# The head of a hybrid decoder kernel: x transposed before it is normalised, 1/rms applied from a row at eviction

## The chip, the cores and the metric

The kernel runs on one core of one Trainium2 chip. The metric is the device time of one execution in microseconds (us), lower is better. An execution that was taken with the hardware profiler gives the rows of this document.

## The reference, cut to what matters

The program is one layer of a hybrid decoder for 256 prompt tokens and 8 x 4 sample tokens, 288 columns in all, at a width of 2048. Everything starts with

```
h    = x * rsqrt(mean(x*x over the 2048) + 1e-6) * g_pre
proj = h @ w_in          # 2048 x (5*2048 + 16 + 5*2048)
```

The first columns of `proj` that the kernel makes are the 2048 of `vb`; then gates, an mLSTM branch and a gMLP branch, two further projections, an output projection and a last RMSNorm follow. All inputs and outputs are float32.

## The kernel before, in words

**Products.** The 104 weight pairs (256 columns each, `w_in`, `w_pb`, `w_pa`, `w_out`) are all done in one way. A pair comes in four chunks of 4 x 128 rows. SyncE loads a chunk into `raw`, ScalarE rounds it to `whi` (L800), VectorE makes the rest `wlo = raw - whi` (L1064), and TensorE does for each of the 4 x 128 rows k and each of the 2 x 128 columns three products over 288 tokens: `whi` by `xh`, `whi` by `xl`, `wlo` by `xh` (L440 to L442). `xh` and `xl` are the rounded upper and the lower part of the transposed, normalised x, 16 pieces (k = 0 to 15) of 128 x 288. They are made once, in the head, while the first pair runs, and used until the last branch.

**The head.** SyncE loads x in four pieces: prompt rows 0 to 127 (1 MB), the samples on 32 partitions, the two halves of prompt rows 128 to 255 (L359 to L362); then weights. TensorE runs idle matmuls (L456, `idle_run`) on the identity. Squares are summed by ScalarE (L817, L820) and VectorE (L1075, L1078); VectorE adds them (L1081, L1084), GpSimd takes the power -0.5 (L1655) into `rstd`. ScalarE (L825) and VectorE (L1093) then multiply x by `rstd`, in quarters of 512 columns, into `hb`; tokens are partitions there, so `rstd` is a scalar of each partition. TensorE transposes `hb` in 128 x 128 blocks, three a k (L474, L475), into PSUM. ScalarE evicts a k times `g_pre` into `xh` (L835); VectorE evicts the same bank once more and subtracts into `xl` (L1106). The first six k are transposed before the first product, the others one by one between the products of k = 1 to 10 (`x_piece`). VectorE's queue has the lower split of chunks 0 to 3 among these.

**Behind the first pair** come the gate sums (32 products, L483 and L484), the second pair with the transposes of `w_s` (L491) in it, and so on. The order of every engine is written out by hand; engines wait for each other by semaphores. GpSimd sets constants and masks at the start (memsets and selects, L1620 to L1651), issues the load of the gate weights `wg` (L1653), takes the power, issues four small loads, waits until all of x is transposed, makes further constants, and loads `wsn`, `bsb`, `lng`, `lnb`.

Of the kernel before, what the change touches and what calls it, by code (L numbers as in the profile page):

```python
# [26 lines left out]
F32 = mybir.dt.float32  # L27
# [5 lines left out]
P = 128  # L33
D = 2048
# [19 lines left out]
SQ = D // 4  # L54
LO = 32
# [43 lines left out]
def build(nc, x_prompt, x_sample, state_C, state_n, state_m, state_conv, g_pre, w_in, b_ig, b_fg,  # L99
# [35 lines left out]
    xpart = fixed("xpart", [P, 3])  # L135
# [14 lines left out]
    xt = a("xt", [P, 3, D])  # L150
    hb0 = a("hb0", [P, 3, D])
    prow = a("prow", [P, 2, P])
    a = Area(phase)
# [118 lines left out]
    def sem(name):  # L272
# [9 lines left out]
    x_norm_a, x_in_rest, x_sum = sem("x_norm_a"), sem("x_in_rest"), sem("x_sum")  # L282
# [4 lines left out]
    x_sq, x_var, x_rstd, x_norm, x_t, x_hi, x_lo = (sem(n) for n in (  # L287
        "x_sq", "x_var", "x_rstd", "x_norm", "x_t", "x_hi", "x_lo"))
# [60 lines left out]
    def x_bank(k):  # L349
        return 2 + k % 6  # L350
# [76 lines left out]
    def _(pe):  # L427
        def chunk(pair, c, slot, free, mh_, ml_, pieces=None):
# [25 lines left out]
        def idle_run(n):  # L454
            for _ in range(n):
                nc.tensor.matmul(ps[:, 7, 0:P], ident[:], ident[:], start=True, stop=True)  # L456

        pe.wait_ge(consts, 1)
        idle_run(28)
        pe.wait_ge(par_in, 64)  # L460
        pe.transpose(ps[:, 6, 0:P], prow[:, 0, :], ident[:])
        pe.transpose(ps[:, 6, P:P + 64], prow[0:64, 1, :], ident[0:64, 0:64]).then_inc(par_t, 1)
        def turn_x(k0, k1):

            for k in range(k0, k1):
# [1347 lines left out]
```

## Time and profile before

| what | us |
|---|---|
| median of 3 runs | 1482.71 |
| lowest and highest of them | 1482.71, 1483.03 |
| the profiled execution, its own time | 1483.09 |
| its span, first to last instruction | 1481.6 |
| TensorE busy | 1466.3 |
| VectorE busy | 880.8 |
| ScalarE busy | 620.1 |
| GpSimd busy | 190.6 |

Times within rows count from the start of the span. PE is TensorE, PEld its weight load, DVE VectorE, ACT ScalarE, POOL GpSimd, SP SyncE. A matmul's recorded duration overlaps that of the next; what one costs is read from start to start. An idle matmul on float32 has two records.

### The profile page before, as it was taken

The page shows a single profiled execution, that of the slowest core. Times are in us where ns is not written, and L with a number is a line of the kernel's source. Part 1 is how long each engine was busy: PE and PEld are TensorE (multiplying, and loading weights), DVE is VectorE, ACT ScalarE, POOL GpSimd, SP SyncE. Part 2 cuts the span into 40 slices and gives each one's busy share as a digit, 9 for nine tenths or more (in the row PEclk, how much of TensorE's full clock was granted, in tenths as well). Part 3 has the DMA queues.
Part 4 walks back from the last instruction along what each step waited for, and adds up shares of the span by engine and source line. Part 5 has one row for each costly group of instructions (what it writes and reads, how often), then busy time and mean ns, then how long its engine had stood idle before and what let it go on. Part 6 is the DMA issues. An engine that isn't in the chain of part 4 may idle for free. (4 is left out here: it accounts for less than half of the span.)

```text
span 1481.6 us, 31209 instructions
## 1 busy us (share of the span) xinstructions
PE 1466.3 (99%) x11131; PEld 1448.1 (98%) x11131; DVE 880.8 (59%) x1451; ACT 620.1 (42%) x869; POOL 190.6 (13%) x340
## 2 busy tenths in 40 slices
PE   9999999999999999999999999999999999999996
PEld 9999999999999999999999999999999999999996
DVE  7756565564434447676767677777767544545444
ACT  6433333333333334444544444544453343333442
POOL 4000000001000000304040404040412100000000
PEclk9999999999999999999999999999999999999998
DMA  7764655557555568696969696979796665655543
GB/s 230 222 160 134 181 154 169 167 145 244 185 171 179 176 188 213 160 297 162 300 167 292 166 296 171 288 184 281 185 277 166 210 184 169 183 174 187 173 157 138
DMA packets 310678, 292.14 MB, mean 197 GB/s; under 512 B 82880, under 2 KB 297608, under 8 KB 309840
## 3 DMA queue, kind: packets, MB, share of 16 engines
q1 hardware_dynamic: 291424, 243.05, 59.1%
q0 software_dynamic: 18960, 48.48, 9.7%
q8 instruction: 24, 0.39, 0.1%
q10 hardware_dynamic: 256, 0.10, 0.0%
q14 instruction: 14, 0.11, 0.0%
HBM read 266.11 MB, written 25.44 MB: 197 GB/s over the span
## 5 line engine op out<-in xcount | busy, mean ns | idle before, releaser
L1064 DVE TENSOR_TENSOR wlo<-raw,whi 128x1024 fp32r<-128x1024 f32 x416 | 507.7, 1223 | 534.2 <-ACT whi L800 529.1
L440 PE MATMUL ps<-xh,whi 128*128 128x288 f32 x2560 | 762.3, 298 | 0.0
L442 PE MATMUL ps<-xh,wlo 128*128 128x288 f32 x2560 | 755.5, 295 | 0.0
L441 PE MATMUL ps<-xl,whi 128*128 128x288 f32 x2560 | 754.5, 295 | 0.0
L800 ACT ACTIVATE whi<-raw 128x1024 fp32r<-128x1024 f32 x416 | 440.4, 1059 | 748.8 <-PE ps L442 718.7
L440 PEld LDWEIGHTS ps<-xh,whi 128*128 128x128 f32 x2560 | 481.4, 188 | 6.9 <-issue 6.2
L442 PEld LDWEIGHTS ps<-xh,wlo 128*128 128x128 f32 x2560 | 480.6, 188 | 0.0
L441 PEld LDWEIGHTS ps<-xl,whi 128*128 128x128 f32 x2560 | 480.3, 188 | 0.2
L441 PE MATMUL ps<-yl,whi 128*128 128x288 f32 x512 | 151.5, 296 | 0.0
L440 PE MATMUL ps<-yh,whi 128*128 128x288 f32 x512 | 150.8, 294 | 0.0
L442 PE MATMUL ps<-yh,wlo 128*128 128x288 f32 x512 | 150.6, 294 | 0.0
L442 PEld LDWEIGHTS ps<-yh,wlo 128*128 128x128 f32 x512 | 96.2, 188 | 0.0
L440 PEld LDWEIGHTS ps<-yh,whi 128*128 128x128 f32 x512 | 96.2, 188 | 0.0
L441 PEld LDWEIGHTS ps<-yl,whi 128*128 128x128 f32 x512 | 96.1, 188 | 0.0
L440 PE MATMUL ps<-mh,whi 128*128 128x288 f32 x248 | 73.5, 296 | 0.0
L441 PE MATMUL ps<-ml,whi 128*128 128x288 f32 x248 | 73.4, 296 | 0.0
L442 PE MATMUL ps<-mh,wlo 128*128 128x288 f32 x248 | 73.1, 295 | 0.0
L1736 POOL DMA_DIRECT2D out_dram<-cst x64 | 36.1, 564 | 219.0 <-DVE cst L1431 214.2
L1361 DVE SCALAR_TENSOR_TENSOR Cin<-Cin,dec_bc,ps 128x512 f32<-128x512 f32 x64 | 46.3, 744 | 0.6
L440 PEld LDWEIGHTS ps<-mh,whi 128*128 128x128 f32 x248 | 46.6, 188 | 0.0
L441 PEld LDWEIGHTS ps<-ml,whi 128*128 128x128 f32 x248 | 46.6, 188 | 0.0
L442 PEld LDWEIGHTS ps<-mh,wlo 128*128 128x128 f32 x248 | 46.6, 188 | 0.0
(341 smaller groups left out, 1073.8 us busy)
## 6 DMA issues: line engine op xcount, KB each, us to landing
raw<-in_w_in_dram SPq DMA_DIRECT2D x320, 512.0 KB, 4.0
raw<-in_w_pb_dram SPq DMA_DIRECT2D x32, 512.0 KB, 3.5
Cin<-in_state_mlstm_C_dram POOLq DMA_DIRECT2D x16, 1024.0 KB, 8.7
Xb<-in_state_mlstm_C_dram SPq DMA_DIRECT2D x256, 64.0 KB, 3.8
out_dram<-Cin POOLq DMA_DIRECT2D x16, 1024.0 KB, 6.0
raw<-in_w_pa_dram SPq DMA_DIRECT2D x32, 512.0 KB, 3.5
raw<-in_w_out_dram SPq DMA_DIRECT2D x32, 512.0 KB, 3.5
bcs<-rows_d POOLq DMA_DIRECT2D x8, 304.0 KB, 3.9
```

The costliest lines, as they stand in the source:

```text
L440: nc.tensor.matmul(out, whi[:, c, kk, cols], mh_[:, k, :], start=(k == 0), stop=False)
L441: nc.tensor.matmul(out, whi[:, c, kk, cols], ml_[:, k, :], start=False, stop=False)
L442: last = nc.tensor.matmul(out, wlo[:, c, kk, cols], mh_[:, k, :], start=False, stop=(k == KT - 1))
L800: nc.scalar.activation(whi[:, c], raw[:, c], ACT.Copy).then_inc(hi_ready, 1)
L1064: nc.vector.tensor_tensor(wlo[:, c], raw[:, c], whi[:, c].bitcast(F32), ALU.subtract).then_inc(lo_ready, 1)
L1361: nc.vector.scalar_tensor_tensor(Cin[:, b], Cin[:, b], dec_bc[:, ds(8 * h + b, 1)], ps[:, NEW_BANK[b % 3], :].rearrange("p (v k) -> p v k" ...
L1736: pool.dma_start(blocks_of(conv_p_v, h, s, g), cst[g:g + 3, 2 * s:2 * s + 2, :]).then_inc(cst_out, 16)
```

## The change

x is transposed as it lands, before anything is known of its mean square. `hb` is gone.

- SyncE loads the first half of prompt rows 128 to 255 ahead of the samples, and the samples in four quarters of 512 columns onto the four groups of 32 partitions (`xs`).
- TensorE: 21 idle matmuls, transposes of k = 0 to 7 of the first 128 rows, 5 idle matmuls, the two transposes of parameters, those of k = 0 to 7 of the second 128 rows, 4 for all the samples, a matmul that adds the four partial sums of squares of a sample (`same_x`), 10 idle matmuls. The transposes of k = 8 to 15 are done in four calls of 4, ahead of the products of k = 2, 4, 6 and 8.
- `rstd` is brought to all partitions as a row of 288: VectorE multiplies the identity by it (`diag`), TensorE multiplies ones by that, ScalarE copies the result to `rbc`.
- VectorE makes `xn` (a ring of four pieces of 128 x 288 in SBUF) from PSUM times `g_pre` times `rbc`, in two instructions, 256 and 32 columns; ScalarE rounds it to `xh`; `xl = xn - xh` is made by VectorE for k = 0 and 1 and by GpSimd for k = 2 to 15.
- The products of a k in the first pair are in the order: four with `xh`, then two with `xl`; their waits are separate.
- VectorE does the memsets that GpSimd did; GpSimd does its later constants, the small loads and `wg` before the power, and `wsn` and `bsb` behind it, ahead of the subtractions; `lng` and `lnb` come behind them.

```
-        sp.dma_start(xt[0:S, 2, :], xs_v).then_inc(x_in[2], 16)
         sp.dma_start(xt[:, 1, HALVES[0]], xp_v[:, 1, HALVES[0]]).then_inc(x_in[1], 16)
+        for q in range(4):
+            sp.dma_start(xs[S * q:S * q + S, :], xs_v[:, SQ * q:SQ * q + SQ]).then_inc(x_in[2], 16)
...
         pe.wait_ge(consts, 1)
-        idle_run(28)
+        idle_run(21)
+        pe.wait_ge(x_in[0], 16)
+        for k in range(8):
+            turn_x(k, 0)
+        idle_run(5)
         pe.wait_ge(par_in, 64)
...
+        pe.wait_ge(x_in[1], 16)
+        for k in range(8):
+            turn_x(k, 1)
+        pe.wait_ge(x_in[2], 64)
+        for n in range(CK):
+            pe.transpose(ps[:, 7, P * n:P * n + P], xs[:, P * n:P * n + P], ident[:])
+        pe.wait_ge(xs_sq, 1)
+        pe.wait_ge(x_made, 3)
+        nc.tensor.matmul(ps[:, 6, 0:1], same_x[:], xpart[:, 3:4], start=True, stop=True).then_inc(xs_sum, 1)
+        idle_run(10)
+
+        def rstd_rows():
...
+            for t, n in enumerate((P, P, S)):
+                pe.wait_ge(x_made, t + 4)
+                last = nc.tensor.matmul(ps[:, 6, P * t:P * t + n], ones8[:], diag[:, P * t:P * t + n],
+                                        start=True, stop=True)
+            last.then_inc(rbc_mm, 1)
+
+        def turn_more(k):
+
+            pe.wait_ge(x_t, k - 6)
+            for kk in (k, k + 1):
+                for t in range(2):
+                    last = pe.transpose(x_prompt_t(kk)[:, P * t:P * t + P], xt[:, t, P * kk:P * kk + P], ident[:])
+            last.then_inc(x_more, 1)
+
+        def first_chunk(c):
+
+            pe.wait_ge(lo_ready, c + 1)
+            for kk in range(CK):
+                k = CK * c + kk
+                if k in (2, 4, 6, 8):
+                    turn_more(k + 6)
+                pe.wait_ge(x_hi, k + 1)
...
+                    nc.tensor.matmul(out, whi[:, c, kk, cols], xh[:, k, :], start=(k == 0), stop=False)
+                    nc.tensor.matmul(out, wlo[:, c, kk, cols], xh[:, k, :], start=False, stop=False)
+                if k < XL_DVE:
+                    pe.wait_ge(x_lo, k + 1)
+                else:
+                    pe.wait_ge(x_lo_p, k + 1 - XL_DVE)
+                for j in range(2):
+                    last = nc.tensor.matmul(ps[:, j, 0:T], whi[:, c, kk, P * j:P * j + P], xl[:, k, :],
+                                            start=False, stop=(k == KT - 1))
...
+        act.wait_ge(x_in[2], 64)
+        nc.scalar.activation(junk_s[:, 0:SQ], xs[:], ACT.Square, accum_out=xpart[:, 3:4]).then_inc(xs_sq, 1)
+        act.wait_ge(xs_sum, 1)
+        nc.scalar.activation(stat[:, 2:3], ps[:, 6, 0:1], ACT.Copy).then_inc(x_sq, 1)
         act.wait_ge(x_in_rest, 16)
-        nc.scalar.activation(hb0[:, 1, QUARTERS[3]], xt[:, 1, QUARTERS[3]], ACT.Square,
+        nc.scalar.activation(junk_s[:, SQ:2 * SQ], xt[:, 1, QUARTERS[3]], ACT.Square,
                              accum_out=xpart[:, 2:3]).then_inc(x_sq, 1)
         split_hi(0, 0, first=True)
...
+        act.wait_ge(rbc_mm, 1)
+        nc.scalar.activation(rbc[:], ps[:, 6, 0:T], ACT.Copy).then_inc(rbc_set, 1)
         for k in range(KT):
...
+            nc.scalar.activation(xh[:, k, :], xn[:, k % 4, :], ACT.Copy).then_inc(x_hi, 1)
+            if k in (1, 5, 9):
                 split_hi(0, k // CK + 1, first=True)
...
         dve.wait_ge(x_rstd, 1)
+        for t, n in enumerate((P, P, S)):
+            nc.vector.tensor_scalar(diag[:, P * t:P * t + n], ident[:, 0:n], rstd[:, t:t + 1], None,
+                                    ALU.mult).then_inc(x_made, 1)
         split_lo(0, 0)
+        dve.wait_ge(rbc_set, 1)
         dve.wait_ge(par_set, 1)
...
+            nc.vector.scalar_tensor_tensor(xn[:, k % 4, 0:TP], x_prompt_t(k), g_at, rbc[:, 0:TP], ALU.mult, ALU.mult)
+            nc.vector.scalar_tensor_tensor(xn[:, k % 4, TP:T], x_sample_t(k), g_at, rbc[:, TP:T], ALU.mult,
+                                           ALU.mult).then_inc(x_t, 1)
...
+        for k in range(XL_DVE, KT):
+            pool.wait_ge(x_hi, k + 1)
+            nc.gpsimd.tensor_tensor(xl[:, k, :], xn[:, k % 4, :], xh[:, k, :].bitcast(F32),
+                                    ALU.subtract).then_inc(x_lo_p, 1)
+        pool.wait_ge(rbc_mm, 1)
```

How the work stands on the engines around it, first TensorE from its first instruction up to the first products. Before:

```order
L456 MATMUL ps<-ident 128x128 [waits consts]
L456 MATMUL ps<-ident 128x128 x27
L461 MATMUL ps<-ident,prow 128x128 [waits par_in]
L462 MATMUL ps<-ident,prow 128x64
L456 MATMUL ps<-ident 128x128 x11
L474 MATMUL ps<-ident,hb_73 128x128 [waits x_norm,x_norm_a]
```

and in the changed kernel, whose line numbers are its own (L473 is the idle matmul, L476 and L492 the transposes, L495 the sum over the sample's quarters, L504 the row of 1/rms, L527 the first product):

```order
L473 MATMUL ps<-ident 128x128 [waits consts]
L473 MATMUL ps<-ident 128x128 x20
L476 MATMUL ps<-ident,xt 128x128 [waits x_in0]
L476 MATMUL ps<-ident,xt 128x128 x7
L473 MATMUL ps<-ident 128x128 x5
L485 MATMUL ps<-ident,prow 128x128 [waits par_in]
L486 MATMUL ps<-ident,prow 128x64
L476 MATMUL ps<-ident,xt 128x128 [waits x_in1]
L476 MATMUL ps<-ident,xt 128x128 x7
L492 MATMUL ps<-ident,xs 128x128 [waits x_in2]
L492 MATMUL ps<-ident,xs 128x128 x3
L495 MATMUL ps<-xpart,same_x 128x1 [waits x_made,xs_sq]
```

24 transposes and the sum stand ahead of the wait for 1/rms, where nothing of x stood before.

ScalarE, from the first square to the first rounding of x. Before:

```order
L817 ACTIVATE hb_73,stat<-xt 128x2048 [waits x_in0,table_in]
L817 ACTIVATE hb_73,stat<-xt 32x2048 [waits x_in2]
L820 ACTIVATE hb_73,xpart<-xt 128x512 [waits x_in_rest]
L800 ACTIVATE whi<-raw 128x1024 [waits raw_landed0]
L825 ACTIVATE hb_73<-xt,rstd 128x512 [waits x_rstd]
```

and in the changed kernel:

```order
L869 ACTIVATE junk_a,stat<-xt 128x2048 [waits x_in0,table_in]
L871 ACTIVATE xn,xpart<-xs 128x512 [waits x_in2]
L873 ACTIVATE stat<-ps 128x1 [waits xs_sum]
L875 ACTIVATE xn,xpart<-xt 128x512 [waits x_in_rest]
L854 ACTIVATE whi<-raw 128x1024 [waits raw_landed0]
L879 ACTIVATE rbc<-ps 128x288 [waits rbc_mm]
```

The copy that waits for TensorE's sum (`xs_sum`) now stands ahead of the last square.

VectorE, from the use of `rstd` on. Before:

```order
L1093 TENSOR_SCALAR hb_73<-xt,rstd 128x512 [waits x_rstd]
L1093 TENSOR_SCALAR hb_73<-xt,rstd 32x512
L1064 TENSOR_TENSOR wlo<-raw,whi 128x1024 [waits hi_ready]
L1093 TENSOR_SCALAR hb_73<-xt,rstd 128x512
L1093 TENSOR_SCALAR hb_73<-xt,rstd 32x512
```

and in the changed kernel (L1110 is the lower split, L1171 and L1172 make `xn`, L1180 `xl`):

```order
L1156 TENSOR_SCALAR diag<-ident,rstd 128x32
L1110 TENSOR_TENSOR wlo<-raw,whi 128x1024 [waits hi_ready]
L1171 SCALAR_TENSOR_TENSOR xn<-ps,par_59,rbc 128x256 [waits par_set,rbc_set]
L1172 SCALAR_TENSOR_TENSOR xn<-ps,par_59,rbc 128x32
L1171 SCALAR_TENSOR_TENSOR xn<-ps,par_59,rbc 128x256
L1172 SCALAR_TENSOR_TENSOR xn<-ps,par_59,rbc 128x32
L1180 TENSOR_TENSOR xl<-xn,xh 128x288 [waits x_hi] x2
L1171 SCALAR_TENSOR_TENSOR xn<-ps,par_59,rbc 128x256
L1172 SCALAR_TENSOR_TENSOR xn<-ps,par_59,rbc 128x32
L1171 SCALAR_TENSOR_TENSOR xn<-ps,par_59,rbc 128x256
L1172 SCALAR_TENSOR_TENSOR xn<-ps,par_59,rbc 128x32
L1110 TENSOR_TENSOR wlo<-raw,whi 128x1024 [waits hi_ready]
```

The lower split of chunk 0 stands between the diagonal and the first `xn`, and that of chunk 1 behind the fourth.

## Rows read from the trace of the kernel before

**Rows 1.** The page, busy time of the engines.
```profile
PE 1466.3 (99%) x11131; PEld 1448.1 (98%) x11131; DVE 880.8 (59%) x1451; ACT 620.1 (42%) x869; POOL 190.6 (13%) x340
```

**Rows 2.** TensorE's waits in the whole span: total us, times, longest.
```profile
PE ps L474 <- ACT hb L825: 0.7, 1, 0.7
PE ps L739 <- DVE vf_o L1598: 0.7, 1, 0.7
```

**Rows 3.** Timeline of TensorE: start, us, instructions, idle time before.
```profile
1.84 8.15 PE L456 MATMUL ps<-ident 128*128 128x128 f32 x56 [1.84 <-POOL ident L1621]
9.83 0.27 PE L461 MATMUL ps<-ident,prow 128*128 128x128 f32 x1
...
10.23 2.72 PE L456 MATMUL ps<-ident 128*128 128x128 f32 x22
13.66 0.42 PE L474 MATMUL ps<-ident,hb 128*128 128x128 f32 x2 [0.70 <-ACT hb L825]
...
16.14 0.38 PE L440 MATMUL ps<-xh,whi 128*128 128x288 f32 x1
...
32.26 0.29 PE L483 MATMUL ps<-xh,wg 128*104 128x288 f32 x1
...
36.47 0.29 PE L440 MATMUL ps<-xh,whi 128*128 128x288 f32 x1
...
39.66 1.04 PE L491 MATMUL ps<-ident,wsn 128*128 128x128 f32 x8
```

**Rows 4.** Timeline of TensorE, 5.8 to 6.8 alone.
```profile
5.59 1.39 PE L456 MATMUL ps<-ident 128*128 128x128 f32 x11
```

**Rows 5.** Timeline of ScalarE.
```profile
8.57 1.89 ACT L817 ACTIVATE hb<-xt 32x2048 f32<-32x2048 f32 x1
...
10.46 0.61 ACT L820 ACTIVATE hb<-xt 128x512 f32<-128x512 f32 x1
10.98 0.18 ACT L820 ACTIVATION_READ_ACCUMULATOR hb<-xt 128x1 f32 x1
...
14.28 1.68 ACT L835 ACTIVATE xh<-ps,par 128x288 fp32r<-128x288 f32 x4
...
43.27 1.06 ACT L800 ACTIVATE whi<-raw 128x1024 fp32r<-128x1024 f32 x1 [9.16 <-DMA raw<-in_w_in_dram]
```

**Rows 6.** Timeline of VectorE.
```profile
9.32 1.23 DVE L1075 SCALAR_TENSOR_TENSOR hb<-xt 128x1024 f32<-128x1024 f32 x1 [3.65 <-DMA xt<-in_x_prompt_dram]
...
11.20 0.22 DVE L1081 SCALAR_TENSOR_TENSOR stat<-xpart 128x1 f32<-128x1 f32 x1
...
12.64 0.87 DVE L1093 TENSOR_SCALAR hb<-xt,rstd 128x512 f32<-128x512 f32 x2 [0.48 <-POOL rstd L1655]
...
15.37 1.77 DVE L1106 SCALAR_TENSOR_TENSOR xl<-ps,par,xh 128x288 fp32r<-128x288 f32 x4
...
29.56 3.50 DVE L1064 TENSOR_TENSOR wlo<-raw,whi 128x1024 fp32r<-128x1024 f32 x3 [0.32 <-ACT whi L800]
```

**Rows 7.** Timeline of GpSimd in the head.
```profile
2.02 0.34 POOL L1627 MEMSET gq<- 128x288 f32 x1
...
5.06 1.06 POOL L1637 TENSOR_SCALAR_AFFINE_SELECT keep_w<-keep_w 128x128 f32<-128x128 f32 x3 [0.23 <-POOL ones L1633]
...
11.72 0.89 POOL L1655 TENSOR_TENSOR rstd<-stat,half 128x3 f32<-128x3 f32 x1 [1.00 <-DVE stat L1084]
...
14.36 0.80 POOL L1660 DMA_DIRECT2D nrow<-in_state_mlstm_n_dram  x1
```

**Rows 8.** Timeline of all engines, 619 to 621: a power beside VectorE.
```profile
619.65 0.75 DVE L1361 SCALAR_TENSOR_TENSOR Cin<-Cin,dec_bc,ps 128x512 f32<-128x512 f32 x1
619.71 1.00 POOL L1745 TENSOR_TENSOR rstd<-stat,half 128x3 f32<-128x3 f32 x1 [12.25 <-DVE stat L1498]
```

**Rows 9.** Stretches of the tail: busy of each engine, granted clock, DMA share, GB/s.
```profile
1468.00:1470.00 2.00, 1.34 (x10) 1.26 (x11) 1.66 (x8) 0.30 (x2) 0.15 (x1) 0.90 0.02 4
1470.00:1472.00 2.00, 0.59 (x3) 0.19 (x1) 1.25 (x3) 0.00 (x0) 0.73 (x1) 0.50 0.01 4
```

More of the change, by code:

```diff
@@ L134, in build @@
     stat = fixed("stat", [P, 3])
-    xpart = fixed("xpart", [P, 3])
+    xpart = fixed("xpart", [P, 4])
     gq = fixed("gq", [P, 3, 96])
@@ L149, in build @@
     a = Area(phase)
-    xt = a("xt", [P, 3, D])
-    hb0 = a("hb0", [P, 3, D])
-    prow = a("prow", [P, 2, P])
+    xt = a("xt", [P, 2, D])
+    xs = a("xs", [P, SQ])
+    xn = a("xn", [P, 4, T])
+    rbc = a("rbc", [P, T])
+    junk_s = xn[:].rearrange("p k t -> p (k t)")
+    assert a.at <= phase + 3 * D * 4
+    a = Area(phase + 3 * D * 4)
+    junk_a = a("junk_a", [P, D])
+    prow = a("prow", [P, 2, P])
+    fold_x = a("fold_x", [P, S])
+    same_x = a("same_x", [P, P])
+    diag = a("diag", [P, T])
+    assert a.at <= phase + 5 * D * 4
+    junk_v = a("junk_v", [P, 3 * SQ])
     a = Area(phase)
@@ L281, in build @@
                                          sem("w_sp_in"), sem("ln_in"))
-    x_norm_a, x_in_rest, x_sum = sem("x_norm_a"), sem("x_in_rest"), sem("x_sum")
+    xs_sq, x_in_rest, x_sum = sem("xs_sq"), sem("x_in_rest"), sem("x_sum")
+    xs_sum, x_made, rbc_mm, rbc_set, x_lo_p = (sem(n) for n in (
+        "xs_sum", "x_made", "rbc_mm", "rbc_set", "x_lo_p"))
     row_out, bc_in, n_step = sem("row_out"), sem("bc_in"), sem("n_step")
@@ L346, in build, with x_prompt_t, x_sample_t @@
     block.__enter__()
[L349 to L350 removed]
+    def x_prompt_t(k):
+        return ps[:, 2 + k // 2 % 4, TP * (k % 2):TP * (k % 2) + TP]
+    def x_sample_t(k):
+        at = P * (k % CK) + S * (k // CK)
+        return ps[:, 7, at:at + S]
     def of_c(b):
@@ L427, in _, with chunk @@
     def _(pe):
-        def chunk(pair, c, slot, free, mh_, ml_, pieces=None):
+        def chunk(pair, c, slot, free, mh_, ml_):
             pe.wait_ge(lo_ready, 4 * pair + (c + 1))
@@ L530, in v_body @@
                 for c in range(CHUNKS):
-                    chunk(V0 + s + 2 * i, c, s, None if first else i, xh, xl,
-                          x_piece if first and s == 0 else None)
+                    if first and s == 0:
+                        first_chunk(c)
+                    else:
+                        chunk(V0 + s + 2 * i, c, s, None if first else i, xh, xl)
                     if first and (s, c) == (0, 3):
@@ L1108, in _ @@
+        for k in range(KT):
+            normalise(k)
+            if k == XL_DVE - 1:
+                for kk in range(XL_DVE):
+                    dve.wait_ge(x_hi, kk + 1)
+                    nc.vector.tensor_tensor(xl[:, kk, :], xn[:, kk, :], xh[:, kk, :].bitcast(F32),
+                                            ALU.subtract).then_inc(x_lo, 1)
+            if k in (3, 7, 11):
+                split_lo(0, k // CK + 1)
         dve.wait_ge(gw_hi, 2)
@@ L1625, in _ @@
         nc.gpsimd.memset(mask8[:], 1.0)
[L1626 to L1634 removed]
+        nc.gpsimd.memset(tri01[:], 1.0)
+        nc.gpsimd.memset(blk01[:], 1.0)
+        step(nc.gpsimd.memset(eye8[:], 0.0))
         def select(out, pattern, base, cm, fill, op=ALU.is_ge):
@@ L1673, in _ @@
                                 channel_multiplier=1).then_inc(consts, 1)
+        pool.dma_start(bg[:, 0:1], b_ig.unsqueeze(1)).then_inc(gb_in, 16)
+        pool.dma_start(bg[:, 1:2], b_fg.unsqueeze(1)).then_inc(gb_in, 16)
+        with nc.allow_non_contiguous_dma(reason="64 values"):
+            pool.dma_start(m0[:], state_m.rearrange("b h -> h b")).then_inc(gb_in, 16)
+        pool.dma_start(nrow[:], state_n.rearrange("b h d -> (b h) d")).then_inc(gb_in, 16)
+        pool.dma_start(wg[:], w_in.rearrange("(k p) n -> p k n", p=P)[:, :, COL_IG:COL_IG + 16]).then_inc(gin, 16)
+        pool.wait_ge(x_var, 1)
+        nc.gpsimd.tensor_tensor(rstd[:], stat[:], half[:], ALU.pow).then_inc(x_rstd, 1)
         pool.dma_start(wsn[:], w_s.rearrange("g t s -> t g s")).then_inc(w_sp_in, 16)
```

144 lines of the change are left out of this document (54 added, 90 removed).

## The prediction

> **What bounds the kernel now.** I read the page first: TensorE is busy for 1466.3 of 1481.6 us [rows 1]. The list of its waits over the whole span has six entries: the first start (1.8), two in the head (0.7 and 0.4 us, before transposes), and three short ones in the last 16 us, the longest again 0.7 [rows 2]. So from the first product (16.14) to the tail the kernel is TensorE's own work, laid end to end. Other engines matter only where they make TensorE wait. The change touches only the stretch before that and the first weight pair, so I then read the timeline of each engine there [rows 3 to 7]. The mark to watch is the start of the gate sums, 32.26 [rows 3]: it is the moment at which the first pair is over. Whatever shift the new kernel has there it keeps to the end, because everything behind it is unchanged and bound by TensorE. Later waits would only come from weight loads. The nearest is the ScalarE split at 43.27 that waited 9.16 us for its weights [rows 5], yet TensorE did not stall there; GpSimd's new order takes the loads of `wsn` and `bsb` out of that crowded stretch, to the time behind the power. I cost it at nothing; what hides it is the lead of the weight loads.
>
> Before 16.14 TensorE runs idle matmuls and waits for others. The chain there is squares of x on ScalarE and VectorE (ScalarE ends at 11.16), sums on VectorE (11.20), the power on GpSimd (11.72), `rstd` used at 12.64 [rows 5 to 7], normalising, then 18 transposes from 13.66 to 16.1 [rows 3].
>
> **The change, step by step.**
> *Where the sum of squares ends.* The samples' square is now 512 instead of 2048 columns: 0.6 instead of 1.9 us [rows 5], a gain on ScalarE of 1.3 us. But its partial sums need a matmul (`xs_sum`), and that stands in TensorE's queue behind fixed work. Idle matmuls are two records each and from 5.6 us on run 0.111 us apart (11 starts in 1.39 us less the 0.27 of one) [rows 4]. In the old kernel 56 records run from 1.84 until the next matmul starts at 9.83 [rows 3]. The new run has 42, 14 fewer, so it ends at 9.83 - 1.55 = 8.28. Then come 8 transposes at 0.11 (to 9.15), 5 idle matmuls (1.11, to 10.25), the two parameter transposes (9.83 to 10.23 before, 0.40, to 10.65), 8 + 4 transposes (1.3, to 11.95) and `xs_sum`, whose result I put at 12.25. The data is there: VectorE's half of x landed at 9.32 with the samples ahead of it and now goes ahead of them [rows 6]. ScalarE copies the sum (0.2, as its 0.18 read of one column [rows 5]), then squares its quarter of x with the read of the accumulator: 10.46 to 11.16 before, 0.70. It ends at 12.25 + 0.20 + 0.70 = 13.15, where it ended at 11.16. So the diagonal's `rstd` comes **2.0 us later**: VectorE has it at 14.64 instead of 12.64. GpSimd is free by then: it had been idle for 1.00 when the power came at 11.72, it loses the memsets from 2.02 to the first select (3 us), and gains two memsets, three selects (three took 1.06) and four DMA issues of at most 0.8 [rows 7]. That makes 12.3 at the latest, and the power is wanted at about 13.7.
>
> *From `rstd` to the first product.* VectorE makes three pieces of the diagonal (under 0.2 each, its one-column sum took 0.22 with the start [rows 6]; to 15.15), then the lower split of chunk 0 (1.14 start to start: 3 in 3.50 [rows 6]) to 16.3. Beside it TensorE sums the diagonal (three matmuls, about 15.5) and ScalarE copies the row (0.5, to 16.0); this is hidden by the split, and if the split were gone it would be 0.3 us shorter. VectorE then normalises piece 0 in two instructions. Four of the old 288-column ones took 1.77, so 0.42 apart, of which 0.12 is not columns; 256 and 32 columns make 0.385 + 0.155 = 0.54. To 16.85, ScalarE's rounding 0.5, and the first product starts at **17.4, that is 1.3 us later** than 16.14.
>
> *TensorE's work in the first pair.* 24 products lie between 36.47 and 39.66, 0.133 apart [rows 3]; 96 of them make 12.8 us, as before. Before, 30 transposes stood between them, 10 k's by 3; 16.14 to 32.26 is 16.1 us, so they cost 3.35, 0.11 each. Now 4 calls of 4 stand there: 16 by 0.11 = 1.75. **Saved: 1.6 us.** The transposes of k 0 to 7 now run in the head beside waits for data, worth nothing there but for their place ahead of `xs_sum`, counted above.
>
> *The supply of x.* VectorE spends 4 x 0.54 + 1.14 = 3.3 us on four k's; TensorE 3.2, or 4.07 while transposes stand between (k 2 to 9). So VectorE keeps up, but for some tenths. ScalarE: 1.68 for four and 1.06 for a split [rows 5], under 2.8, hidden. GpSimd now has 14 subtractions of two 128x288 tiles. The trace has no such instruction. From below it is a memset of that size, 0.34 [rows 7]. From above it is the power at 1.00, GpSimd's dearest operation on data [rows 8], with the memset's columns on top (0.34 less a fixed 0.1 or so): about 1.2. I take 0.7, between them, because its opcode is the power's (which has the larger fixed part) and its columns are the memset's. The Trainium skill, GPSIMD Engine Reference, section 3.1, has a two-input elementwise operation at about 2.6 cycles per element; an estimate from it is 0.63 us and a fixed part, and the sum would be the same. The first subtraction (k = 2) can start when VectorE has done two pieces of 0.54, two own subtractions of 0.42, one more piece, and ScalarE the rounding behind its chunk-1 split: about 19.4. It is ready at 20.1; TensorE wants it at 19.9. From there 0.7 is under TensorE's 0.8 a k. I count 0.3 us of waiting at k = 2 and 0.4 in pieces where VectorE is the slower: **lost, 0.7 us**. Each subtraction also holds a slot of the ring `xn` (four), which VectorE waits for; at 0.7 that hides under VectorE's own work.
>
> *Sum:* +1.3 - 1.6 + 0.7 = **+0.4 us**. The pair ends at 32.6. Against the profiled execution (1483.09 for its span of 1481.6) that is 1483.5; the median of the three runs shown, 1482.71, lies 0.4 below that execution, and so the forecast in such medians is **1483.1**.
>
> **Rivals.** *The two engines shut each other out* (0.25). While VectorE's split of a weight chunk reads two tiles of SBUF, GpSimd's subtraction can't start. The split of chunk 1 then begins just ahead of the subtraction for k = 2 and holds it from 19.4 to 20.6; so it is ready at 21.3 and TensorE waits 1.4 instead of 0.3. Two more blocks of 1.1 come while GpSimd gains 0.1 us a k: 0.2 more. End: 17.4 + 14.5 + 1.6 = 33.5, +1.2 us, 1483.9. For it speaks a weak sign: a power on GpSimd that began 0.06 us after a VectorE operation took 1.00 [rows 8] where the one of the head with VectorE idle took 0.89 [rows 7]; against it, that GpSimd was not held for the 0.75 us of that operation. The Trainium skill, SBUF — State Buffer, section "Who interferes with whom", says just this of a VectorE instruction with two SBUF inputs against a GpSimd one that reads SBUF; no run here shows it in full.
>
> *Slower: GpSimd sets the pace* (0.15). Its 14 pieces start at 19.4, and TensorE wants the last at 17.4 + 14.5 - 0.3 = 31.6. So above (31.6 - 19.4) / 14 = 0.87 us a piece it decides, and the pair ends at 19.4 + 14 x piece + 0.3, plus 3.4 with the shutting out. At 1.2, the bound above, that is 36.5, +4.2 us, 1486.9; at 1.0 with the shutting out 37.1, +4.9, 1487.6. Slower by over 0.2% it is from 1.1 us alone, or 0.86 with the shutting out. For it: the opcode's only rows are 0.89 and 1.00 for 3 columns. Against it: selects and memsets are cheap.
>
> *TensorE's clock falls in the head* (0.10). TensorE now idles from about 14.5, with three small matmuls between, to 17.4, and again at k = 2; before it had 0.7 and 0.4. In the tail the granted clock was 0.90 and then 0.50, the lower level of 1.2 GHz, over 1468 to 1472, after gaps of 0.3 to 0.7 us and one-column matmuls [rows 9]. A slow phase at the start shows in the spacing: of the 56 records 37 fit behind 5.6 us at 0.111, so 19 took 3.8 us, 0.2 each. A second such phase costs 19 x 0.09 = 1.7 us. +0.4 + 1.7 = +2.1, 1484.8; with the stalls of the case before, +3.
>
> *Faster* (0.12). If `xs_sum` were not what the sum of squares waits for (TensorE's early work faster than I count, x late by nothing), the first product would be at 15.4 to 16; with little waiting the pair ends at 30.1 to 31.5, -2.2 to -0.8, 1480.5 to 1481.9. Nothing in the head can give more than that, as 30.1 has every wait gone.
>
> **How the numbers follow.** 0.38 for the sum as it stands. A measurement of this kernel can tell about 0.2%, 3 us, from no change. Within it lie the sum, the shutting out, most of the faster case and nearly half of the clock's: 0.76. Slower by more: GpSimd's pace 0.15 and the rest of the clock's, 0.21. Faster by more: 0.03 for what I have not seen. The range leaves out half of the faster case below and the upper part of GpSimd's pace above: 1481.5 to 1487.0.
>
> **What would show it.** The row of the first product (17.4; a start under 16.5 says the chain over `xs_sum` is wrong); ScalarE's square of the quarter ending at 13.15; GpSimd's subtraction (0.7; 0.87 is the point) and whether it starts while a weight split runs; TensorE's waits in 17 to 33, 0.7 in sum; the gate sums at 32.6; the granted clock 1.00 to 33. A later shift that differs from the one at the gate sums would prove wrong that all behind is unchanged.

## The result, and the profile after

| what | before | changed |
|---|---|---|
| median of 14 runs each, one chip | 1482.91 | 1485.80 |
| lowest to highest | 1482.68 to 1483.33 | 1484.40 to 1486.64 |
| the profiled execution | 1483.09 | 1486.44 |
| its span | 1481.6 | 1484.0 |

The changed kernel is slower: ratio 1.0019, 95% interval 1.0011 to 1.0026, or +2.9 us. That is at the edge of the 0.2% that I had called no change. The range of the prediction (1481.5 to 1487.0) holds it; the likeliest case (+0.4, 1483.1) missed by 2.7.

TensorE's timeline of the changed kernel, up to the third row of products and from the gate sums on:

```profile
1.84 7.30 PE L473 MATMUL ps<-ident 128*128 128x128 f32 x42 [1.84 <-POOL ident L1698]
8.98 1.04 PE L476 MATMUL ps<-ident,xt 128*128 128x128 f32 x8
...
12.75 0.28 PE L495 MATMUL ps<-xpart,same_x 128*128 128x1 f32 x2
12.89 2.48 PE L473 MATMUL ps<-ident 128*128 128x128 f32 x20
15.74 1.16 PE L504 MATMUL ps<-diag,ones 128*128 128x128 f32 x6 [0.38 <-DVE diag L1156]
...
18.65 0.37 PE L527 MATMUL ps<-xh,whi 128*128 128x288 f32 x1 [1.74 <-ACT xh L882]
...
22.49 0.53 PE L534 MATMUL ps<-xl,whi 128*128 128x288 f32 x2 [1.05 <-POOL xl L1740]
...
34.94 0.29 PE L542 MATMUL ps<-xh,wg 128*104 128x288 f32 x1
```

The first product starts at 18.65 where it started at 16.14 [rows 3]: **+2.51**. From there to the gate sums it is 16.29 us, where it was 16.12: +0.17. Behind them come 1449.1 us of span, before 1449.3: nothing is lost there. So in this pair of executions the span grew by 2.4, and nearly all of it lies ahead of the first product. In medians it is the same: the span is 1483.9 in the 14 runs, against 1481.3 to 1481.4 in the runs of the kernel before that were taken beside the experiments. Two runs of those sets, one of experiment four (1945.72) and one of the kernel before beside it (2079.28), had mean clocks of 0.69 and 0.64 and are left out of every figure. What the time adds to the span is 1.5 us in both, but 1.9 to 2.5 in five of the 14 runs of the changed kernel, the profiled one among them.

The chain ahead of the first product. ScalarE:

```profile
9.79 0.63 ACT L871 ACTIVATE xn<-xs 128x512 f32<-128x512 f32 x1 [1.45 <-DMA xs<-in_x_sample_dram]
...
13.07 0.17 ACT L873 ACTIVATE stat<-ps 128x1 f32<-128x1 f32 x1 [2.55 <-PE ps L495]
13.13 0.62 ACT L875 ACTIVATE xn<-xt 128x512 f32<-128x512 f32 x1
13.65 0.19 ACT L875 ACTIVATION_READ_ACCUMULATOR xn<-xt 128x1 f32 x1
...
18.06 0.99 ACT L882 ACTIVATE xh<-xn 128x288 fp32r<-128x288 f32 x2 [0.71 <-DVE xn L1172]
```

and VectorE, from the landing of the last piece of x:

```profile
10.80 0.69 DVE L1143 SCALAR_TENSOR_TENSOR junk_v<-xt 128x512 f32<-128x512 f32 x1 [1.05 <-DMA xt<-in_x_prompt_dram]
...
13.88 0.22 DVE L1146 SCALAR_TENSOR_TENSOR stat<-xpart 128x1 f32<-128x1 f32 x1 [2.38 <-ACT xn L875]
...
15.31 0.93 DVE L1156 TENSOR_SCALAR diag<-ident,rstd 128x128 f32<-128x128 f32 x3 [0.48 <-POOL rstd L1733]
16.16 1.20 DVE L1110 TENSOR_TENSOR wlo<-raw,whi 128x1024 fp32r<-128x1024 f32 x1
17.39 0.48 DVE L1171 SCALAR_TENSOR_TENSOR xn<-ps,par,rbc 128x256 f32<-128x256 f32 x1
...
20.57 1.22 DVE L1110 TENSOR_TENSOR wlo<-raw,whi 128x1024 fp32r<-128x1024 f32 x1
...
24.36 1.47 DVE L1110 TENSOR_TENSOR wlo<-raw,whi 128x1024 fp32r<-128x1024 f32 x1 [0.36 <-ACT whi L854]
```

All of x was there at 10.80, and ScalarE had nothing to do from 10.5 to 13.07 but wait for TensorE's sum of the samples. The quarter's square stood in its queue behind that copy, and VectorE waited 2.38 for the quarter. `rstd` was used at 15.31 (12.64 before [rows 6]).

GpSimd, the first subtraction in its timeline:

```profile
20.67 1.77 POOL L1740 TENSOR_TENSOR xl<-xn,xh 128x288 fp32r<-128x288 f32 x1 [3.91 <-ACT xh L882]
```

All fourteen in the groups by line and form (busy us, mean ns of one, idle time before them):

```profile
L1740 POOL TENSOR_TENSOR xl<-xn,xh 128x288 fp32r<-128x288 f32 x14 | 13.8, 1013 | 3.9 <-ACT xh L882 3.9
```

Nine of them, those that start before 30 us, in the view of the tile (min/median/max ns, first and last start):

```profile
L1740 POOL TENSOR_TENSOR xl<-xn,xh x9: 795/807/1770, 20.7 to 28.8; 128x288 fp32r<-128x288 f32 x9
```

A subtraction takes 0.80 us, but the first took 1.77: VectorE's split of a weight chunk had begun at 20.57, a tenth before it, and ended at 21.79. Three of the fourteen are so long, each beside one of the three splits. In the other two cases the split paid as well, 1.47 instead of 1.22, since it found a subtraction in flight.

### The profile page after: what moved, and what is told of

It reads as the page before. It is cut to its first block and busy times, and to the rows that moved or that the text cites. A ratio compares the mean times of both kernels' runs of the same rounds, so it can differ in the third digit from the quotient of the medians.

```text
span 1484.0 us, 31221 instructions
## 1 busy us (share of the span) xinstructions
PE 1466.4 (99%) x11121; PEld 1447.8 (98%) x11121; DVE 883.6 (60%) x1478; ACT 616.5 (42%) x867; POOL 199.8 (13%) x340
## 5 line engine op out<-in xcount | busy, mean ns | idle before, releaser
L1110 DVE TENSOR_TENSOR wlo<-raw,whi 128x1024 fp32r<-128x1024 f32 x416 | 508.1, 1224 | 533.9 <-ACT whi L854 528.7
L457 PE MATMUL ps<-xh,whi 128*128 128x288 f32 x2528 | 751.9, 297 | 0.0
L459 PE MATMUL ps<-xh,wlo 128*128 128x288 f32 x2528 | 746.0, 295 | 0.0
L458 PE MATMUL ps<-xl,whi 128*128 128x288 f32 x2528 | 745.1, 295 | 0.0
L457 PEld LDWEIGHTS ps<-xh,whi 128*128 128x128 f32 x2528 | 475.4, 188 | 6.9 <-issue 6.2
L459 PEld LDWEIGHTS ps<-xh,wlo 128*128 128x128 f32 x2528 | 474.7, 188 | 0.0
L458 PEld LDWEIGHTS ps<-xl,whi 128*128 128x128 f32 x2528 | 474.3, 188 | 0.2
```

The source lines that it names most:

```text
L457: nc.tensor.matmul(out, whi[:, c, kk, cols], mh_[:, k, :], start=(k == 0), stop=False)
L458: nc.tensor.matmul(out, whi[:, c, kk, cols], ml_[:, k, :], start=False, stop=False)
L459: last = nc.tensor.matmul(out, wlo[:, c, kk, cols], mh_[:, k, :], start=False, stop=(k == KT - 1))
L1110: nc.vector.tensor_tensor(wlo[:, c], raw[:, c], whi[:, c].bitcast(F32), ALU.subtract).then_inc(lo_ready, 1)
```

## The experiments

Each kernel below has 11 runs. The first four shared a chip (before: median 1482.84), the next four another (1482.93), the last four a third (1482.88). The time between the first product and the gate sums is called the pair.

**One.** Is it the splits that hold GpSimd up? The splits of chunks 1 to 3 subtract a tile of PSUM instead of `whi`; the kernel leaves out the right lower half of these weights.

```
-            nc.vector.tensor_tensor(wlo[:, c], raw[:, c], whi[:, c].bitcast(F32),
-                                    ALU.subtract).then_inc(lo_ready, 1)
+            other = whi[:, c].bitcast(F32)
+            if free_port:
+                other = ps[:, 6, 0:PW].unsqueeze(1).broadcast_to([P, CK, PW])
+            nc.vector.tensor_tensor(wlo[:, c], raw[:, c], other, ALU.subtract).then_inc(lo_ready, 1)
...
-                split_lo(0, k // CK + 1)
+                split_lo(0, k // CK + 1, free_port=True)
```

> The changed kernel, but VectorE's lower split of chunks 1 to 3 of the first pair reads its second input from PSUM (a bank that is at rest) and so only one tile of SBUF; this leaves out the right lower half of those weights. If VectorE and GpSimd shut each other out over two SBUF inputs, none of the 14 subtractions takes 1.77 us any more, all take 0.80, the splits take 1.2 and not 1.47, TensorE's waits at k = 2 and k = 8 (1.2 and 0.3) fall to 0.4 in sum at most, and the time falls by 0.9 to 1.3 us. If the long subtractions have another cause (a first use, descriptors of the loads issued before), three of 1.77 stay and the time stays within 0.3.

Measured 1484.65 (1484.29 to 1486.10), ratio 1.0013 [1.0003, 1.0022]. The groups of GpSimd and VectorE:

```profile
L1742 POOL TENSOR_TENSOR xl<-xn,xh 128x288 fp32r<-128x288 f32 x14 | 11.0, 816 | 5.8 <-ACT xh L882 5.8
...
L1113 DVE TENSOR_TENSOR wlo<-raw,ps 128x1024 fp32r<-128x1024 f32 x3 | 3.6, 1217 | 0.7 <-ACT whi L854 0.7
```

With one operand in PSUM no subtraction is long any more (mean 816 ns, was 1013), and no split (1217 ns, was 1383 for the three). TensorE no longer waits for `xl`. The mechanism is shown; its price is not, for in the profiled execution something else took the place of the waits. The windows, the column after the busy times being the granted clock:

```profile
16.00:18.00 2.00, 0.26 (x2) 0.19 (x2) 1.97 (x6) 1.05 (x3) 0.00 (x0) 1.00 1.11 280
18.00:20.00 2.00, 2.00 (x12) 2.00 (x12) 1.91 (x7) 1.77 (x4) 0.15 (x1) 0.69 1.02 305
20.00:22.00 2.00, 2.00 (x11) 1.98 (x10) 2.00 (x6) 0.76 (x2) 1.41 (x2) 0.50 1.06 372
22.00:24.00 2.00, 2.00 (x17) 2.00 (x16) 1.64 (x6) 1.90 (x4) 1.67 (x3) 0.96 0.90 246
```

TensorE was busy for 0.26 of the 2 us from 16 to 18; then the granted clock went to 0.50, the lower level of 1.2 GHz, and the products from 18.90 to 22.15 came 0.24 apart instead of 0.133. The pair took 16.11. In the profile of the changed kernel the same gap had a clock of 1.00 behind it. So the clock's fall comes in some executions and not in others. What the shutting out costs where the clock stays up is read in experiment seven.

**Two to four.** What holds up the sum of squares? The `xs_sum` matmul ahead of the transposes of the second rows (two), the quarter's square ahead of the copy (three), 12 instead of 21 idle matmuls at the start (four).

```
+        pe.wait_ge(xs_sq, 1)
+        pe.wait_ge(x_made, 3)
+        nc.tensor.matmul(ps[:, 6, 0:1], same_x[:], xpart[:, 3:4], start=True, stop=True).then_inc(xs_sum, 1)
         pe.wait_ge(x_in[1], 16)
         for k in range(8):
             turn_x(k, 1)
```

> The changed kernel, but the matmul that adds the samples' four sums stands ahead of the second rows' transposes in TensorE's queue (behind the parameters' transposes). If the first product is late because that matmul stands behind fixed work, ScalarE's copy of the sum moves from 13.07 to about 11.6, its last square ends at about 12.4, rstd is used 1.4 us earlier than 15.31, the first product is at about 17.2 instead of 18.65 and the time falls by 1.2 to 1.5 us. If the landing of x sets the start (last part at 10.8), it moves by under 0.3.

```
         act.wait_ge(x_in_rest, 16)
         nc.scalar.activation(junk_s[:, SQ:2 * SQ], xt[:, 1, QUARTERS[3]], ACT.Square,
                              accum_out=xpart[:, 2:3]).then_inc(x_sq, 1)
+        act.wait_ge(xs_sum, 1)
+        nc.scalar.activation(stat[:, 2:3], ps[:, 6, 0:1], ACT.Copy).then_inc(x_sq, 1)
```

> The changed kernel, but ScalarE squares its quarter of x before it copies the samples' sum. If the wait for the sum with the square queued behind it is on the path, the sum of squares on VectorE starts at 13.25 instead of 13.88, the first product and the time are 0.6 us earlier. If another thing ends the wait, no change within 0.2.

```
-        idle_run(21)
+        idle_run(12)
```

> The changed kernel with 12 instead of 21 idle matmuls at the start. If the idle run pushes the samples' sum back, TensorE is 9 matmuls (1.0 us at 0.111 a record half, up to 3.3 us where the clock is still at its lower level) earlier at that sum: rstd 1.0 to 1.6 us earlier, the first product at 17.0 to 17.6, the time 1 to 1.5 us less, and the runs lie closer together than the 2.2 us between the lowest and the highest of the changed kernel, because the slow phase at the start no longer decides. If fewer idle matmuls leave the clock at its lower level for longer, the transposes and the first products run at twice their spacing and it is 1 us or more slower.

| edit | copy of the sum | first product | pair | median (lowest to highest) | ratio, 95% |
|---|---|---|---|---|---|
| none | 13.07 | 18.65 | 16.29 | 1485.80 | 1.0019 [1.0011, 1.0026] |
| two | 11.75 | 17.65 | 16.31 | 1484.62 (1483.77 to 1486.08) | 1.0013 [1.0004, 1.0022] |
| three | 12.89 | 17.87 | 16.30 | 1484.91 (1483.85 to 1485.76) | 1.0013 [1.0004, 1.0022] |
| four | 11.47 | 17.05 | 16.30 | 1483.85 (1483.74 to 1485.05) | 1.0008 [0.9999, 1.0018] |

Each brings the first product forward, by 1.0, 0.8 and 1.6 us, and the time by 1.2, 0.9 and 1.95; the pair stays as it is, to 0.02 us. Of three's 0.8, 0.17 is no gain of the edit: the idle run at the start happened to end earlier in that execution (8.81 instead of 8.98). The median spans fall by 0.8, 0.8 and 1.55 us, which fits the first product; the rest of four's 1.95 is an excess of the time over the span that four does not have (see *Open*). So x's sum of squares did wait for TensorE's queue, and the idle matmuls at its head, that do nothing, were on the path: nine fewer of them are worth the most. In four 7 of the 10 runs have a mean clock of 0.995 or less, though its profiled execution shows 1.00 throughout the head and the pair.

**Five and six.** All three edits, 4 instead of 10 idle matmuls behind the sum, and in five also 7 idle matmuls behind the diagonal's, in the gap before the first product.

```
             last.then_inc(rbc_mm, 1)
+            idle_run(7)
```

> The changed kernel with the sum's matmul ahead of the second rows' transposes, ScalarE's quarter squared before the copy of the sum, 12 idle matmuls at the start, 4 instead of 10 behind the transposes and 7 more behind the matmuls of the diagonal (1.55 us, inside TensorE's gap of 1.75 us before the first product). By the queue theory the sum of squares starts at 11.7 instead of 13.88 and the first product is at 16.3 to 16.6; the first pair still takes 16.3 us, with 1.2 to 1.5 of waiting for GpSimd; the gate sums start at 32.6 to 32.9 and the time is 0.3 to 0.7 us above the kernel before. With the gap filled no run has products at the lower clock in the first pair, so the runs lie within 1 us. If the start is bound by the row of 1/rms or by the landing of x instead, the first product stays at 17.0 or later.

> The same without the 7 idle matmuls behind the diagonal. If the gap ahead of the first product is what lets TensorE's clock fall in some runs, some of these executions show products 0.24 us apart for about 3.4 us near the start of the pair and are 0.8 to 1.6 us slower than the others, and the spread is above 1 us; the fastest are as fast as those with the idle matmuls. If the clock does not depend on the gap, both kernels have the same times and spread.

Five: 1483.41 (1483.04 to 1483.84), ratio 1.0003 [0.9994, 1.0012]; first product 16.68, gate sums 32.97, pair 16.29. Its timeline of TensorE, at the first product and at the one wait behind it:

```profile
14.77 1.81 PE L473 MATMUL ps<-ident 128*128 128x128 f32 x14
16.68 0.37 PE L528 MATMUL ps<-xh,whi 128*128 128x288 f32 x1
...
20.52 0.53 PE L535 MATMUL ps<-xl,whi 128*128 128x288 f32 x2 [1.05 <-POOL xl L1741]
...
32.97 0.29 PE L543 MATMUL ps<-xh,wg 128*104 128x288 f32 x1
```

The sum of squares is no longer late for TensorE's queue: it starts at 11.90, once the last quarter of x, which landed at 11.09, has been squared. In the profiled executions of seven, ten and eleven x landed at 10.83 to 10.86 and the first product is at 16.42 to 16.44. So in these versions, where the clock stays up, the landing of x sets the start.

Six: 1483.45 (1483.28 to 1484.40), ratio 1.0004 [0.9995, 1.0013]; first product 17.24, gate sums 33.55, pair 16.31. The median is that of five, but the slowest four of the 11 runs are at 1483.93 to 1484.40, where all 11 of five lie within 0.8 us. The profiled execution (1484.01) shows two falls of the clock, again in the column after the busy times:

```profile
12.00:14.00 2.00, 2.00 (x11) 2.00 (x10) 1.49 (x8) 1.06 (x1) 1.84 (x3) 0.50 1.12 304
14.00:16.00 2.00, 1.50 (x9) 1.39 (x7) 1.16 (x3) 0.41 (x1) 0.53 (x1) 0.69 1.11 277
16.00:18.00 2.00, 0.76 (x6) 0.79 (x7) 1.91 (x6) 1.24 (x3) 0.00 (x0) 1.00 1.10 278
18.00:20.00 2.00, 2.00 (x14) 1.98 (x13) 2.00 (x6) 1.48 (x3) 0.74 (x1) 0.66 1.04 306
```

The first fall is in the head, ahead of the gap. The matmuls of the diagonal run in it, and ScalarE's copy of the row starts at 15.54, in five at 14.97; the first product is at 17.24 instead of 16.68. This fall costs. The second, behind the gap, has products 0.24 apart from 18.50 to 22.1 and costs nothing: no wait for `xl` is left, and the pair takes 16.31 as against 16.29. The 7 idle matmuls stand behind the diagonal and can't prevent the first fall: nine, below, has them and its profile shows that fall too (0.50 from 12 to 15, first product 17.26). Behind the gap the clock fell in the profiled executions of one, six and twelve, which lack the 7 idle matmuls, and in none of the six kernels that have them; but the changed kernel, two, three and four lack them as well, and there it did not fall. That the filled gap prevents the second fall is therefore likely and not shown. The mean clocks of the runs don't settle it: at 0.995 or less are 7 of 11 runs in six, none in five and seven, but 9 of 44 in eight to eleven, which all have the 7 idle matmuls. Of the 2.9 us the clock is not a main term.

What is left of five over the kernel before is 0.5 us in time. In the profiled executions, whose spans differ by 0.3, it is 0.54 in the first product and 0.17 in the pair, less 0.4 behind.

**Seven.** Five with the splits of one: the price of the shutting out where the clock stays up.

> The early and warm kernel with the lower splits of chunks 1 to 3 reading one tile of SBUF and one of PSUM (this leaves out the right lower half of those weights). Against the early and warm kernel only the shutting out of GpSimd is gone: TensorE's waits in the pair fall from 1.2 to 1.5 to at most 0.5 us, the pair takes 14.9 to 15.3 us, and the time is 1.0 to 1.4 us less. If the waits had a second cause (VectorE as the bound of the pair), the time falls by under 0.5.

1482.52 (1482.34 to 1483.28), ratio 0.9997 [0.9988, 1.0006]; first product 16.44, gate sums 31.87. The pair takes 15.43 instead of 16.29, and the median time is 0.89 less, a little short of the 1.0 to 1.4 expected. **The shutting out costs 0.9 us.**

**Eight.** A way round it: VectorE makes `xl` for k = 2 too, before its split of chunk 1, and ScalarE rounds chunk 1 before it copies the row.

```
-XL_DVE = 2
+XL_DVE = 3
...
+        split_hi(0, 1, first=True)
         act.wait_ge(rbc_mm, 1)
...
-            if k in (1, 5, 9):
+            if k in (5, 9):
```

> The early and warm kernel with VectorE making the lower part of k = 2 too, ahead of its split of chunk 1, and ScalarE rounding chunk 1 before the row of 1/rms. The first wait for GpSimd (1.0 at k = 2) goes; by the order of the shutting out it comes back at k = 3 as 0.8 to 1.0, since the split of chunk 1 now runs when that piece is ready; GpSimd has one piece less. Time 0.1 to 0.5 us below the early and warm kernel. If it is 1 us less, the wait at k = 2 was worth its full length and nothing takes its place.

1484.05 (1483.57 to 1484.51), ratio 1.0007 [0.9998, 1.0016]: slower than five, a miss. ScalarE's timeline:

```profile
14.27 1.06 ACT L855 ACTIVATE whi<-raw 128x1024 fp32r<-128x1024 f32 x1 [0.85 <-DMA raw<-in_w_in_dram]
15.35 0.41 ACT L881 ACTIVATE rbc<-ps 128x288 f32<-128x288 f32 x1
```

The chunk had not landed; the rounding waited for it and ended at 15.33, and the row behind it came 0.4 later than in five. The first product was at 17.06, and three waits for GpSimd of 1.1 in sum were left. In this execution the clock had fallen in the head as well (0.50 from 12 to 14), and TensorE's instruction behind the diagonal's matmuls started at 15.15, as far ahead of the row's copy as in five (14.77 and 14.97). So in this profile either of the two alone would have made the row late. The times speak for the rounding: 10 of the 11 runs are slower than every run of five.

**Nine to twelve.** Is it single late pieces of `xl`, or GpSimd's pace? The products with `xl(k)` two k later (nine, on five), VectorE making k = 13 and 15 (ten, on five), both (eleven), both on the changed kernel (twelve).

```
+                for m in ([k - LAG] if k < KT - 1 else range(k - LAG, KT)):
+                    if m >= 0:
+                        low_wait(m)
+                        low(m)
...
+            if k in XL_LATE:
+                dve.wait_ge(x_hi, k + 1)
+                nc.vector.tensor_tensor(xl[:, k, :], xn[:, k % 4, :], xh[:, k, :].bitcast(F32),
+                                        ALU.subtract).then_inc(x_lo, 1)
...
-        for k in range(XL_DVE, KT):
+        for k in (m for m in range(XL_DVE, KT) if m not in XL_LATE):
             pool.wait_ge(x_hi, k + 1)
```

> The version with the early sum and 7 idle matmuls behind the diagonal (first product 16.68, first GpSimd piece 18.69, gate sums 32.97, 1483.41), with one edit: in the first pair TensorE does the two products of xl(k) two k later, behind the products of xh(k + 2). Theory A, TensorE waits only for single late pieces of xl (1.05 at k = 2, 0.43 at k = 12): both waits are covered by two k of other work (1.6 us), the pair takes 16.68 + 14.55 = 31.2 and with small waits 31.5: -1.4 us, 1482.0. Theory B, GpSimd sets the pace of the whole pair: its 14 pieces take 13.78 from 18.69, so the last xl is there at 32.47 whatever order TensorE has, and the gate sums begin at 32.7 to 32.8: -0.2 us, 1483.2; the waits then move to the end of the pair.

> The same version, with one edit: VectorE makes xl for k = 13 and 15 as well, GpSimd 12 pieces. Theory A (single late pieces): the wait at k = 2 stays, that at k = 12 stays: no more than 0.2 us gained, 1483.2 to 1483.4. Theory B (pace): GpSimd's last piece ends 1.55 earlier, the wait of 0.43 at k = 12 stays at first, the rest is bound by TensorE: at most 0.3 us gained, 1483.1. The two differ little here; the run is the other half of the next one.

> Both edits, the lag of two k for the products with xl and VectorE making k = 13 and 15. Theory B (GpSimd's pace is what binds once its lateness at k = 2 is there): the last GpSimd piece ends at 30.9, nothing waits any more, gate sums at 31.3 to 31.6, -1.4 to -1.7 us, 1481.7 to 1482.0, below the kernel before (1482.93) and without leaving anything out. Theory A gives the same number as with the lag alone. If TensorE now waits for xh instead (the ring of four pieces of xn makes VectorE wait for GpSimd), gate sums at 32.3 or later.

> The changed kernel as it is (late sum), with the same two edits. If the loss has two parts that add, the start (+2.5) and GpSimd's pieces (+1.5 of waits), the second part goes: first product still at 17.7 to 18.7, gate sums 14.7 to 14.9 behind it, 32.4 to 33.6; 1484.2 to 1484.6, 1.2 to 1.6 below the changed kernel's 1485.8. If the clock falls in TensorE's gap before the first product (products 0.24 apart for 3 us) some of the runs lie 1 to 1.5 higher, since nothing waits any more that could hide it.

| run | first product | gate sums | pair | median (lowest to highest) | ratio, 95% |
|---|---|---|---|---|---|
| nine | 17.26 | 33.48 | 16.22 | 1483.25 (1483.08 to 1484.71) | 1.0003 [0.9994, 1.0012] |
| ten | 16.42 | 33.29 | 16.87 | 1483.88 (1483.66 to 1484.52) | 1.0008 [0.9999, 1.0017] |
| eleven | 16.44 | 33.49 | 17.05 | 1484.30 (1483.83 to 1485.42) | 1.0010 [1.0001, 1.0019] |
| twelve | 17.86 | 34.91 | 17.05 | 1486.35 (1485.39 to 1487.37) | 1.0023 [1.0014, 1.0032] |

Nine is as the pace had it: the time falls by 0.2 at most, not by 1.4. GpSimd's fourteen pieces follow each other without a gap, and the gate sums start 0.4 behind the end of the last:

```profile
19.27 13.79 POOL L1754 TENSOR_TENSOR xl<-xn,xh 128x288 fp32r<-128x288 f32 x14 [4.68 <-ACT xh L896]
```

That the first product is at 17.26 and not at 16.68 comes with the fall of the clock in the head (see six) and not with the edit. The wait of 1.05 for `xl` is gone, and in its place TensorE waits for `xh`, 0.25 at 19.24 and 0.47 at 29.69. Ten, eleven and twelve are misses: taking two pieces off GpSimd cost 0.5 us (ten against five), 1.05 (eleven against nine) and, with the lag, 0.55 (twelve against the changed kernel), where I had expected up to 1.7 gained. VectorE's timeline in eleven shows why:

```profile
29.30 0.89 DVE L1198 TENSOR_TENSOR xl<-xn,xh 128x288 fp32r<-128x288 f32 x1 [0.51 <-ACT xh L896]
30.11 0.47 DVE L1185 SCALAR_TENSOR_TENSOR xn<-ps,par,rbc 128x256 f32<-128x256 f32 x1
...
31.81 0.61 DVE L1198 TENSOR_TENSOR xl<-xn,xh 128x288 fp32r<-128x288 f32 x1 [0.51 <-ACT xh L896]
```

To make `xl(13)` VectorE waits 0.51 for ScalarE to round it, then takes 0.89 beside GpSimd, and only then makes `xn(14)`, at 30.11; in five it began `xn(14)` at 28.93. GpSimd and TensorE (0.59 at 31.27) now wait for `xh`. So in the last k's the chain through VectorE and ScalarE was nearly as late as GpSimd. In twelve's profile the granted clock falls too (0.70 and 0.50 from 18 to 22).

## Why the prediction was right or wrong

Right: the range, and that the change makes no difference of over 3 us. With +2.9 instead of +0.4 this was close, and luck has a share in it: 0.1 us more would have been over that mark. In the working, right are: that everything behind the gate sums is bound by TensorE and keeps the shift (1449.1 against 1449.3); that the sum of squares now waits for `xs_sum` in TensorE's queue, and the quarter's square behind its copy (experiments two to four); that an early weight load or GpSimd's new order costs nothing later; the subtraction's size, 0.7 predicted, 0.80 measured, 0.78 from start to start; that GpSimd starts 2.0 us behind the first product (20.67 - 18.65; predicted 19.4 - 17.4).

The likeliest case put the gate sums at 32.6 and they came at 34.94 in the profiled execution. The 2.3 us are two terms that were sized too small.

*The start: +1.3 predicted, +2.51 measured.* Step by step:

- The idle run was to end at 8.28 and ended at 8.98: +0.7. I had taken the slow spacing at the start (19 records in 3.8 us) as fixed. It isn't: behind the 42 records the next instruction came at 8.98, 8.94, 8.81, 8.20 and 8.17 in the five profiled kernels that have this run. So this term has a spread of 0.8 us from one execution to the next. I took one execution's value as a constant.
- From there to the square's end it went as worked out: 13.84, predicted 13.15, the same +0.7. `rstd` was used at 15.31 (14.64).
- The diagonal took 0.85 up to the split's start, and I had put under 0.2 for each of its three pieces, 0.5 in sum: +0.35. I priced 128 columns by a row of one column.
- The split took 1.23 to the first `xn` (1.14 predicted), and `xn` and the rounding 1.26 (1.1).

*The pair: 15.2 predicted, 16.29 measured.* The step that was mis-sized is "from there 0.7 is under TensorE's 0.8 a k", with 0.7 us of waiting in all. A subtraction alone is under it, at 0.78 from start to start. With the splits the mean is not: three pieces of 1.77 make the fourteen take 13.76 us, 0.98 each, above the 0.87 that I had named as the point from which GpSimd decides. They follow each other without a gap from 20.67 to 34.43, and the gate sums start 0.5 behind. This is the rival to which I gave only 0.25; its working put 16.1 between first product and gate sums (33.5 - 17.4). Undone, the pair takes 15.43 (seven). Against 96 products and 16 transposes without a wait, 14.5, that is 0.9 for the other latenesses of x, where I had put 0.7. What I held against the shutting out, a power that ran beside a VectorE operation with little delay [rows 8], was no counter-example: that VectorE operation has one of its two tiles in PSUM (`dec_bc` is a single column), and three columns are soon read. The Trainium skill, SBUF — State Buffer, section "Who interferes with whom", has it that a VectorE instruction with two SBUF inputs contends with a GpSimd one that reads SBUF, and that whoever has the shared pair keeps it for the whole instruction. By that rule the trace agrees: 1.77 beside a split and 0.80 without; the split itself 1.47 where it found a subtraction in flight; and 0.80 for all with one input in PSUM.

*The clock* (0.10, at +1.7 on top): it did not fall in the profiled execution of the changed kernel. It fell behind the gap in those of one, six and twelve, and in the head in those of six, eight and nine. The fall behind the gap cost nothing (six), since the products are slow in the very stretch in which TensorE would have waited for `xl`; the fall in the head put the first product 0.6 us back (17.24 and 17.26 as against 16.68). Of the changed kernel's 14 runs three have a mean clock of 0.995, and these have the three shortest spans (1482.9 to 1483.4). One order stands out in the 13 profiled executions of the changed kernel and the experiments: the clock fell in exactly those in which the first idle run ended soonest, at 8.17 and 8.20 of the five with 21 idle matmuls (the others 8.81 to 8.98), and at 6.15, 6.16 and 6.21 of the eight with 12 (the others 6.51 to 7.12). That was found afterwards, and why it should be so is open. The clock is a source of spread rather than a cause of the 2.9.

*The sign.* +2.9 is, in spans, 2.6: 2.5 of start and 0.2 of pair, less a little behind. The 1.6 that 14 transposes less should save went back whole: 0.9 to the shutting out (five against seven), 0.9 to the other latenesses of x.

*Open.* In five of the 14 runs the time exceeds the span by 1.9 to 2.5 us instead of 1.5. An excess of over 1.8 is found in all five kernels with 21 idle matmuls at the start (18 of their 58 runs) and in none of the eight others (0 of 87) nor in the kernel before, which has 28. I have no mechanism for that. It doesn't move the medians of what lies outside the span, but it moves the median of the time by some tenths. Not tried: more than four slots of `xn`, so that VectorE and ScalarE could run ahead; and what makes the start's slow spacing longer or shorter. No version that computes everything beat the kernel before; the nearest are five and nine (ratio 1.0003 each), and the intervals of four, six, eight and ten hold 1 as well.

## What to carry to other kernels

When a small cross-partition sum is put on TensorE, look at what stands ahead of it in the queue: idle matmuls that fill time in one schedule are on the path in the next. Before work is handed to GpSimd beside VectorE, list the VectorE instructions with two SBUF inputs that run in that stretch, and count each as holding GpSimd for its whole length (here 1.77 us instead of 0.80); with one input in PSUM the block was gone. Moving two of GpSimd's fourteen pieces to VectorE made the pair longer and not shorter: where three engines hand pieces round in a ring of four, taking one piece over adds its handover to the taker's chain.

## What the runs showed of the hardware

- The slow spacing of TensorE's matmuls at the start (about 0.19 us instead of 0.111) does not last equally long in every execution: from 5 to 7 us of the span TensorE had 9 and 11 records in the two microseconds of the kernel before, 6 and 8 in those of the changed kernel, 10 and 11 in experiment one, whose TensorE queue is the same there. The profile gives a granted clock of 1.00 throughout.
- The shutting out goes both ways: VectorE's 128x1024 split 1.22 alone and 1.47 behind a subtraction; its 128x288 subtraction 0.46 alone (experiment one, mean of two) and 0.89 beside GpSimd.
- The granted clock can fall to 0.50 for some 3 us in a head with gaps, in some executions of a kernel and not in others: from about 18.7 to 22.1 us behind a gap of 1.7 us in the profiled executions of one, six and twelve, and from 11.5 or 11.8 to 15 us in those of six, eight and nine, where TensorE had waited for 0.8 and 0.7 to 0.9 us between 8.4 and 10.7. With seven idle matmuls in the gap the later fall was seen in none of six profiled executions, the earlier one in two.
- A mean clock over the whole run hides such a fall: nine's profiled run, with 3 us at 0.50, is listed at 0.996, as are runs of the kernel before.
